# Where the scalar engine copies a block's inputs in the state-space loop: ahead of the output tokens, or behind them and the decays

## The reference, cut to what matters

```python
def step(h, u_chunk):
    bu = jnp.einsum('btgs,gps->btgp', u_chunk.astype(jnp.complex64), b_bar)
    a = jnp.broadcast_to(lam_bar, bu.shape)
    _, xs = lax.associative_scan(_ssm_combine, (a, bu), axis=1)
    xs = xs + powers[None] * h[:, None]
    y = jnp.einsum('btgp,gsp->btgs', xs, cmat).real
    return xs[:, -1], y
...
def glu_out(y, g):
    y = jax.nn.gelu(y.astype(g.dtype))
    ya, yb = jnp.split(y @ w_glu + b_glu, 2, axis=-1)
    return ((ya * jax.nn.sigmoid(yb)) * jax.nn.silu(g)) @ w_out
```

## Time and profile before

| What | Value |
|---|---|
| Median of 3 runs (lowest, highest) | 1571.24 us (1564.13, 1583.61) |
| Time of the profiled execution | 1564.13 us |
| Its span | 1562.3 us |
| PE busy, share of the span | 1476.8 us, 95% |
| DVE busy | 951.8 us, 61% |
| ACT busy | 379.3 us, 24% |
| POOL busy | 490.8 us, 31% |
| Mean traffic of the transfers | 199 GB/s |

### The profile page before, as it was taken

How to read it: one execution, slowest core, us unless ns; L and a number is a source line. 1 busy time by engine, 2 the same in 40 slices (tenths; PEclk the granted TensorE clock), 3 DMA queues, 4 the chain that set the end, 5 groups by cost and what they waited for, 6 DMA issues and landing times.

```text
span 1562.3 us, 26034 instructions
## 1 busy us (share of the span) xinstructions
PE 1476.8 (95%) x10184; PEld 1098.6 (70%) x10184; DVE 951.8 (61%) x1693; ACT 379.3 (24%) x910; POOL 490.8 (31%) x462
## 2 busy tenths in 40 slices
PE   5999999999899889999988999999999899999998
PEld 3444456665544368876766788888888788888887
DVE  6849276677699989868778565542351143433374
ACT  1123243443200031235544110000211011232311
POOL 0149999999898049711110000000000000000000
PEclk8999999999999989999999999999999999999999
DMA  9597887787789716689995725432342342434530
GB/s 398 166 263 235 199 233 210 198 214 207 196 272 293 256 31 176 243 298 330 329 317 194 316 114 209 160 163 108 144 152 108 121 149 81 162 142 154 242 148 28
DMA packets 69605, 310.89 MB, mean 199 GB/s; under 512 B 15360, under 2 KB 19584, under 8 KB 44928
## 3 DMA queue, kind: packets, MB, share of 16 engines
q1 hardware_dynamic: 35024, 219.17, 38.8%
q0 software_dynamic: 26160, 65.59, 17.1%
q10 hardware_dynamic: 8320, 24.73, 4.5%
HBM read 263.41 MB, written 46.01 MB: 198 GB/s over the span
## 4 chain that ended last, share of the span: by engine, by line
PE 50%; DVE 3%; DMA 1%; issue 1%; ACT 1%; SPq 0%; ACTq 0%; DVEq 0%
PE bank L978 23%; PE bank L1385 11%; PE bank L1601 4%; PE bank L1270 3%; PE bank L1503 2%; PE bank L1314 2%; PE bank L1337 1%; DMA arena<-in_glu 1%; PE bank L1290 1%; PE bank L1349 1%; PE bank L1326 1%; PE bank L1561 0%; PE bank L1548 0%; PE bank L1527 0%; DVE gate L3075 0%
## 5 line engine op out<-in xcount | busy, mean ns | idle before, releaser
L978 PE MATMUL bank<-arena,ring 128*128 128x256 f32 x960 | 208.5, 379 | 0.0
L978 PEld LDWEIGHTS bank<-arena,ring 128*128 128x128 f32 x960 | 182.4, 190 | 24.8
L978 PE MATMUL bank<-gate,ring 128*128 128x256 f32 (+1 forms) x640 | 194.9, 467 | 4.5 <-DVE gate L2954 3.4
L978 PEld LDWEIGHTS bank<-gate,ring 128*128 128x128 f32 x640 | 122.4, 192 | 76.5 <-issue 62.7
L978 PE MATMUL bank<-ht,ring 128*128 128x256 f32 (+1 forms) x544 | 175.1, 481 | 0.1
L978 PEld LDWEIGHTS bank<-ht,ring 128*128 128x128 f32 x544 | 102.5, 190 | 69.8 <-issue 60.6
L1385 PE MATMUL bank<-arena 128*128 128x256 f32 x576 | 128.7, 382 | 3.1 <-DVE pw L2794 3.1
L1385 PEld LDWEIGHTS bank<-arena 128*128 128x128 f32 x576 | 109.9, 192 | 18.4 <-issue 3.5
L3052 DVE SCALAR_TENSOR_TENSOR arena<-arena,col 128x256 f32<-128x256 f32 x44 | 21.3, 484 | 85.9 <-ACTq L2129 84.1
L1270 PE MATMUL bank<-xc,ring 128*128 128x256 f32 x256 | 68.5, 403 | 1.6 <-issue 1.6
L2422 DVE TENSOR_SCALAR ht<-ht,arena 128x256 f32<-128x256 f32 (+1 forms) x64 | 63.9, 999 | 2.3
(11 more groups left out here) (484 smaller groups left out, 2759.7 us busy)
## 6 DMA issues: line engine op xcount, KB each, us to landing
ring<-in_w_up SPq DMA_DIRECT2D x22, 1024.0 KB, 4.7
ring<-in_mod_tail SPq DMA_DIRECT2D x16, 1024.0 KB, 6.3
arena<-s_b_powers SPq DMA_DIRECT2D x16, 1024.0 KB, 9.7
ring<-in_glu SPq DMA_DIRECT2D x16, 1024.0 KB, 8.3
arena<-in_glu SPq DMA_DIRECT2D x16, 1024.0 KB, 9.2
arena<-s_b_rows POOLq DMA_DIRECT2D x24, 512.0 KB, 11.0
arena<-s_power_rows POOLq DMA_DIRECT2D x24, 512.0 KB, 11.9
s_b_powers<-arena POOLq DMA_DIRECT2D x24, 512.0 KB, 4.8
```

Of the source, the lines that this page charges most:

```text
L978: mm = pe.matmul(psum[2 * (u % 2) + m][:, 0:mv.free_size()], ring[:, sl, k, m * P:(m + 1) * P], mv, start=(kg == 0 and k == 0), stop=(kg = ...
```

## The change

One call of ACT moves down in its loop, from ahead of `tokens(b)` to behind `decays(b+2)`, and its own wait for `y_done` goes, since `tokens(b)` waits for the same value.

```diff
             for b in range(NB5):
                 if b:
                     back(b - 1)
-                if b + 2 < NB5:
-                    act.wait_ge(y_done, b + 1)
-                    u_block(b + 2)
                 tokens(b)
                 if b + 2 < NB5:
                     decays(b + 2)
+                    u_block(b + 2)
                     gate_copy(b + 2)
                 if b + 3 < NB5:
                     kfs(b + 3)
```

## The result

Twenty runs each gave a median of 1578.68 us for the changed kernel (1572.65 to 1594.4) and 1571.99 us for the kernel before (1564.13 to 1589.64). The time lies in the forecast range and on the forecast side. The size, 14.3 us, was too large by more than the interval, and 8.2 us is only just inside the 8 to 24 us that the forecast gave as its own range. The profiled execution took 1577.71 us, with a span of 1575.9.

What follows compares the result with a forecast made beforehand. PE was taken to pace the loop. Waits of 12.1 us at the boundaries and 2.2 at the last, plus 4 for the clock, less 4 for pauses, gave 14.3 us: 1585.5 us from a median of 1571.2, range 1572 to 1603.

Steps and rivals of the forecast that it cites:

- PE paces the loop and the copy's slack is 1.5 us: Loop: PE busy 153.69 of 169.00 us; at the first boundary `u_block` ends 1.5 us before PE starts `inputs`.
- (1): ACT's dropped wait for `y_done`: costs and brings nothing, since `tokens` waits for the same value and the burst starts unchanged.
- (4): `tokens` and `decays` come 0.53 us sooner; counted as 0, bounds -0.5 us to 0.
- (5): Other copies, stores and loads around the loop, and the chain behind it: keep their distances or move along; counted as 0.
- (2): Block boundaries before the last: `inputs` starts 3.40 us after the burst's start, PE waits at eleven; 12.1 us in all.
- (3): Last boundary: `inputs(15)` starts 2.52 us later, so DVE's last scan starts 2.2 us later, all of which shows.
- (6), the clock: PE's clock in the loop: new pauses bring 2 to 3 falls to half clock, 4 us; bounds 0 and 22 us.
- (6), the pauses: PE's 9.2 us of issue pauses in the loop shrink as PE waits: -4 us; bounds 0 and -9.2.
- third rival: Issue pauses in the loop take up the new waits, all 9.2 us vanish, no clock falls: 5.1 us, 1576.3 us; chance 0.16.
- first rival: Clock falls at each new wait in the loop, 1.6 us each, 14 times: 36.7 us, 1607.9 us; chance 0.06.
- The second: Rival: transfers pace the loop, so new waits lie in lost time; only 2.2 us left, 1573.4 us; chance 0.07.
- The fourth: Rival: PE really needs `tokens` first, so putting it first speeds the loop by 7.4 us: 1563.8 us; chance 0.01.

Runs made afterwards that it cites:

- e6_light_after: The changed order with loads of tables bm and cp cut from 1 MB to 32 KB in later blocks; ratio 1.0028 to the kernel before.
- e5_light: The kernel before, old order, with loads of tables bm (from block 3) and cp (from block 5) cut from 1 MB to 32 KB; ratio 0.9911 to the kernel before.
- a0_after: The changed kernel run once more, for a second profile; ratio 1.0031 (1.0001 to 1.0061) to the kernel before.

## Why the prediction was right or wrong

- *PE paces the loop and the copy's slack is 1.5 us*: right. All 14 boundaries show the wait.
- *(1), (4), (5)*: right, as far as shown. ACT's burst starts at `y_done` as before; nothing came sooner for PE.
- *(2), 12.1 us*: the distance that sets a wait was right, 3.48 us against 3.40. The sum of the boundaries was not: I let the pauses of boundaries 3, 8 and 9 cover the wait there. The changed kernel waited 1.2 us at those too, 15.6 us in all, because the pauses had gone. With nothing else going on the whole of (2) and (3) costs 19.4 us of loop (`e6_light_after` against `e5_light`), not 14.3.
- *(3), 2.2 us*: right, 2.24 in profiles; by time not resolved.
- *(6), the clock, +4 us*: wrong for waits of this size. One fall before, one after (one and two in the second profiles); 0 net, or little. One in five pauses was too small a sample to scale from.
- *(6), the pauses, -4 us*: the step that failed. Measured by the loop, pauses and what follows them went from 14.7 us to 3.6 (16.0 to 5.0 in the second profiles): -11 us. I had the right mechanism as third rival, at a chance of 0.16, and argued against it that a pause lies anywhere in a turn. That does not matter: a line has 0.8 us more to arrive in wherever its place is. It also was worth more than the 9.2 us of visible idle time that I had taken as its bound.

So 19.4 - 11.1 = 8.2 us of loop (before rounding), where I had 14.3. That is no second proof, since both numbers are taken from the same four loops; what stands by itself is that the difference by time with cut loads, 18.4 us, is so much larger than the 8.2 with full ones. That the time fell inside the forecast range, which was widened for the scatter of the runs, is in part luck: two terms of (6) were wrong, and (2) was too small by 3.5 us. The third rival's 5.1 us is inside the interval, near its lower edge. The first rival (the clock) needed longer waits. The second (transfers pace the loop) is half true in a way I had not thought of: no table was late, but PE's own instructions were. The fourth (`tokens` first helps) shows nowhere.

## What to carry to other kernels

An empty list of waiters says that a step is in time, not that it may be moved: measure its slack on the two timelines, and multiply by the turns. Before adding up new waits, look at what idle time of cause "issue" the engine already has; if it stands at a fixed distance in the instruction stream and the transfers are near full, expect it to shrink when the engine waits elsewhere, so that an added wait costs less than its length. A view of the transfers in a stretch of 0.1 us ahead of such a pause shows whether a packet of instructions has just started there. In such a loop bytes are worth cutting even if no load is ever waited for: 2 MB a turn less were worth 14 us.

## What the runs showed of the hardware that I had not expected

- PE's pauses in a loop with transfers at a share of 0.95 stand at places 126.3 matmuls apart in its stream, the same places in every run though not all of them in each, 0.2 to 2.3 us long, and are all gone at a share of 0.61.
- All 65 such pauses end 1.2 to 1.7 us after a packet of 16 KB on the queue of instructions has landed. The packet takes 1.1 us (median); under load it starts late, 3.7 us after PE has passed the place before, against 1.2 us with the tables' loads cut. It starts only after that passing at all 21 places looked at in the kernel before and at 18 of 21 in `e5_light`, so there PE had no whole line in hand beyond the one that it was using.
- A wait of 3.43 us in each turn of 17 us cost another 3.9 us of half clock each time (granted clock 0.50 in both windows behind it), while waits of 1.2 us in each turn of 11 us cost none. Between them lies 2.40 us, with a fall in two profiles and without one in three.
- The scatter of the executions is not these pauses: `e6_light_after`, whose profile has none, spread over 12.7 us in twelve executions, `a0_after` over 13.4.
